# The first layer's gate: its last feature tile in two token halves, and an earlier split of the convolution's second weight tile

## The chip, the cores and the metric

One core of a Trainium2 chip runs the whole program. The metric is the device time of one execution in microseconds (us). The kernel before took 1762.61 us, the median of three runs from 1762.31 to 1763.01. The engines are TensorE (PE: matmuls, with weight loads in a queue of their own, PEld), VectorE (DVE), ScalarE (ACT), GpSimd (POOL) and SyncE (SP, which starts the DMA transfers). Each runs its own program in order, and they meet only through semaphores.

## The reference

The reference is a block with two attention branches and then two layers of a second block, on 512 tokens with 1024 features. The change lies at the end of the first of these two layers and the start of the next one's convolution:

```python
        f = sq_relu_mlp(rmsnorm_2(x, g[2]), w_mlp_up[i], w_mlp_down[i])
        x = x + rmsnorm_2(f, g[3])
        gate = jax.nn.sigmoid(rmsnorm_2(x, g[4]) @ w_ple_gate[i])     # 1024 x 1024
        e = (p[i] @ w_ple_proj[i]) * gate
        x = x + rmsnorm_2(e, g[5])
    # layer 1 then begins with rmsnorm_2(x, g[0]) @ w_conv_in (1024 x 3072)
```

`rmsnorm_2` divides each token by the root of the mean of its squares over all 1024 features. So `e` must be complete, in all features, before any token of `x` can be updated, and the convolution's matmuls begin only after that.

## The kernel before

**Layout.** Activations lie with the features on the 128 partitions and the 512 tokens along the free axis. 1024 features are 8 such tiles of 128x512 (`KT` = 8, `S` = 512, `P` = 128); `wt(k)` is tile k of the work buffer. `TOKENS` (L504) names the two token halves of 256 columns.

**Matmuls.** Float32 operands are split into a high and a low part (`fp32r`), and a product is three matmuls: high by high, high by low, low by high (`three`, L813 on; the matmuls are L816, L817 and L818). A weight unit is 1024 rows by 256 columns, in SBUF 128x2048. It comes in by one DMA, ACT copies out the high part, DVE subtracts it to get the low part ("the split"), and PE then makes two tiles of outputs from it (m = 0 and 1), each from 8 steps k of three matmuls. Raw and split weights have two slots each, used in turn. So the split of unit u waits until unit u-2 has been used up (`tile_done` against `pl.freed`), and the load of unit u waits until unit u-2 is split. A tile is made in one of four PSUM banks; `tile_done` counts finished tiles, `tile_read` counts those that have been read.

**The gate of layer 0** has four weight units (`ple_gate0`, 0 to 3). PE (`embed_gate`, L1279) makes units 0 and 1 in `first_units`, and units 2 and 3 in `project` (L921), a hardware loop of one pass; unit 3 goes tile by tile, all of m = 0 and then all of m = 1. For each tile DVE multiplies by the token's scale (`scaled`, L1999), ACT takes the sigmoid (L1848), DVE multiplies the embedding tile by it (L2593), ACT squares the product (L1424), and POOL adds the squares up (`sum_squares`, L2699; each addition is L2709). The eighth square goes around POOL: PE multiplies POOL's sum of seven by a matrix of ones (`begin_statistics`, L937, the matmul is L958) and then adds the eighth (`end_statistics`, L941, the matmul is L943), so that every partition has the sum. `keep_array_busy` (L947, the matmul is L949) issues filler matmuls whose result nobody reads: one between the two and five behind them. These matmuls are plain float32, and each leaves two records in the trace.

**What follows.** ACT loads the table for logarithm and exponential and turns the sum into the scale (`make_rstd`, L1480; L1483 and L1485). DVE and ACT then update x and make the inputs of the convolution (`add_normed`, L2025, in the order `CONV_NORM_ORDER`, L490; `norm_input`, L1431). The first tile goes in token halves. PE's `first_units` takes each tile as it comes, from both of the convolution's first weight units (`conv_in`, 0 and 1), first five steps k of both in turn (`FIRST_UNITS`, L496).

**The split of `conv_in` 1.** It is done in two halves of 1024 columns, so that PE can begin on the lower four steps k early. `conv_in` 1 uses the slot of `ple_gate0` 3, the gate's last unit. On ACT the first half is done in two quarters (`split_quarter`, L1874), of which the first waits until the gate's last unit is used up; they lie before and behind the sigmoid of the last tile. On DVE it comes when all eight gated tiles are done (`split_half`, L2598). The second half stands later, in the orders of the update.

The order of all this on each engine is written out by hand, in the program's order of instructions.

Of the kernel before, what the change touches and what calls it, by code (L numbers as in the profile page):

```python
# [21 lines left out]
P = 128  # L22
# [171 lines left out]
def hybrid_block_kernel(nc, ins, out):  # L194
# [4 lines left out]
    with ctx:  # L199
# [3 lines left out]
        def sem(name):  # L203
            return ctx.enter_context(nc.semaphore(name))
# [43 lines left out]
        def wt(i):  # L248

            return work[:, bass.ds(i * S, S)]  # L250
# [66 lines left out]
        conv_hi = sem("conv_hi")  # L317
        conv_ready = sem("conv_ready")
        gained = sem("gained")
        head_x = sem("head_x")  # L320
        head_hi = sem("head_hi")
        head_scaled = sem("head_scaled")
# [477 lines left out]
        def _(pe):  # L800
# [120 lines left out]
            def project(name, passes, x, ready=None, first=0):  # L921

                with pe.Fori(first, passes) as i:
                    for j in range(2):
                        unit(Place(tab, name, j, i, 2, passes), KT, 256, 2, x, ready if j == 0 else None, by_tile=j == 1)
# [15 lines left out]
            def end_statistics():  # L941
                pe.wait_ge(sq_done, n["squares"])
                nc.tensor.matmul(banks[7][:, :], ones, sq[:, (n["squares"] - 1) % 2, :], start=False, stop=True)\  # L943
                    .then_inc(stat_done, 1)
                n.add("stat")

            def keep_array_busy(*columns):  # L947
                for cols in columns:
                    nc.tensor.matmul(banks[6][:, 0:cols], ones, rope[:, 0:cols], start=True, stop=True)  # L949
# [329 lines left out]
            def embed_gate(layer):  # L1279
                embed_project(f"ple_gate{layer}", layer)  # L1280
                first_units(f"ple_gate{layer}", n.add("in", KT) - KT)
                if layer == 0:
                    project(f"ple_gate{layer}", 2, from_a, first=1)
                    begin_statistics()
                    keep_array_busy(S)
                    end_statistics()
                    keep_array_busy(S, S, S, S, S)
                    return

                x_tiles = iter(range(KT))  # L1290
                addends = iter(range(KT))

                def turn_x(tiles):
                    for _ in range(tiles):
                        turn_out(X + next(x_tiles))

                def turn_addend(tiles):
                    for _ in range(tiles):
                        k = next(addends)
                        pe.wait_ge(gained, k + 1)  # L1300
                        turn_out(EG + k)

# [12 lines left out]
                tokens_half(pl, 1, range(KT // 2))  # L1315
                turn_addend(1)
                tokens_half(pl, 1, range(KT // 2, KT))

                done = n.add("squares", KT)
                for half in range(2):  # L1320
                    pe.wait_ge(gained, KT + half)
                    turn_out(EG + KT - 1, half)
                    if half == 0:
                        pe.wait_ge(sq_added, n.add("sq", KT - 2))
                        pe.wait_ge(rstd_ready, n["stat"])
                        pe.wait_ge(sq_done, done)
                        token_sums(0, (0, 1, 2), pl)
                        token_sums(1, (0, 1), pl)
                    else:
                        pe.wait_ge(sq_done, done + 1)  # L1330
                        token_sums(1, (2,), pl)

            def tokens_half(pl, half, k_tiles):

# [18 lines left out]
            def token_sums(half, parts, pl):  # L1353

                at = token_sums_at(pl, half)
                for part in parts:
                    squares = (ssum[:, :], sq[:, 1 - LAST_SQUARE, :], sq[:, LAST_SQUARE, :])[part]
                    for a in (2 * half, 2 * half + 1):
                        mm = nc.tensor.matmul(at[:, a:a + 1], squares[:, a * P:(a + 1) * P], ones[:, 0:1],
                                              start=part == 0 and a == 2 * half, stop=part == 2 and a == 2 * half + 1)  # L1360
                if part == 2:
                    mm.then_inc(stat_done, 1)
# [17 lines left out]
        def _(act):  # L1380
# [23 lines left out]
            def split_half(name, j, half):  # L1404

                pl = Place(tab, name, j)
                cols = slice(half * UNIT // 2, (half + 1) * UNIT // 2)
                if name == "sb_qk" and half == 0:
                    act.wait_ge(half_landed, 16)
                else:  # L1410
                    act.wait_ge(raw_landed[pl.slot], pl.landed)
                if pl.freed is not None:
                    act.wait_ge(tile_done, pl.freed)
                nc.scalar.activation(wsp[:, pl.slot, 0, cols], raw[:, pl.slot, cols], ACT.Copy)\
                    .then_inc(w_hi if half else half_hi, 1)
# [416 lines left out]
            def embed_gate(layer):  # L1832
                name = f"ple_gate{layer}"
                for j in range(4):
# [11 lines left out]
                    def sigmoid(m):  # L1846
                        act.wait_ge(tile_read, pl.tile + m + 1)
                        nc.scalar.activation(tmp[:, 2 + m, :], tmp[:, m, :], ACT.Sigmoid).then_inc(gate_out, 1)  # L1848
# [22 lines left out]
                        act.wait_ge(ln_done, n["stat"])  # L1871
                        nc.scalar.activation(rstd_tok[:, tiles], rstd_tok[:, tiles], ACT.Exp, scale=-0.5).then_inc(rstd_ready, 1)

                    def split_quarter(quarter):  # L1874
                        following = Place(tab, "conv_in", 1)
                        if quarter == 0:
                            act.wait_ge(raw_landed[following.slot], following.landed)
                            act.wait_ge(tile_done, following.freed)
                        cols = slice(quarter * UNIT // 4, (quarter + 1) * UNIT // 4)
                        mm = nc.scalar.activation(wsp[:, following.slot, 0, cols], raw[:, following.slot, cols], ACT.Copy)  # L1880
                        if quarter == 1:
                            mm.then_inc(half_hi, 1)

                    if layer == 0 and j == 3:
                        sigmoid(0)
                        square_gated(0)
                        split_quarter(0)
                        sigmoid(1)
                        split_quarter(1)
                        square_gated(1)  # L1890
                        table("natural_log_exp_and_others")
                        break
                    if layer == 1 and j == 3:
                        sigmoid(0)
# [53 lines left out]
        def _(dve):  # L1948
# [623 lines left out]
            def embed_gate(layer):  # L2572
                name = f"ple_gate{layer}"
                for j in range(4):
                    pl = Place(tab, name, j)
                    if j == 0:
                        third_after_norm(name)
                        wait_rstd()
                    elif j > 1:
                        ahead(name, j)  # L2580
                    late = j == 3
                    scaled(tmp[:, 0, :], pl, 0)
                    if not late:
                        scaled(tmp[:, 1, :], pl, 1)
                    for m in range(2):
                        if late and m and layer == 1:
                            last_halves(pl)
                            return
                        if late and m:
                            scaled(tmp[:, 1, :], pl, 1)  # L2590
                        dve.wait_ge(gate_out, n.add("gate"))
                        k = 2 * j + m
                        V.tensor_tensor(wt(k), wt(k), tmp[:, 2 + m, :], ALU.mult).then_inc(gated, 1)  # L2593
                        if layer == 1:
                            dve.wait_ge(gated, KT + k + 1)
                            V.tensor_scalar(wt(EG + k), wt(k), col(G_NORM2 + 48 + 40 + k), None, ALU.mult).then_inc(gained, 1)
                dve.wait_ge(gated, KT * (layer + 1))
                split_half("conv_in", 1, 0)  # L2598
                add_normed(0, G_NORM2 + 40, G_NORM2 + 48, "conv_in")

            def last_halves(pl):
                k = KT - 1
# [178 lines left out]
```

## Time and profile before

| | before |
|---|---|
| device time, median of 3 runs | 1762.61 us (1762.31 to 1763.01) |
| the profiled execution, whole | 1762.93 us |
| its span, first to last instruction | 1761.2 us |
| TensorE matmul busy | 1738.8 us, 99% |
| VectorE busy | 1038.4 us, 59% |
| ScalarE busy | 740.9 us, 42% |
| GpSimd busy | 166.9 us, 9% |
| mean granted TensorE clock | 0.997 of full speed |

Busy time is what an engine spent in instructions, as a share of the span. Times in a timeline are from the span's start. Matmuls are pipelined: their records overlap, and the time that one costs in a row of them is the distance from start to start. An idle time in brackets is that of the engine just before the instruction, with what ended it.

### The profile page before, as it was taken

The page shows a single profiled execution, that of the slowest core. Times are in us where ns is not written, and L with a number is a line of the kernel's source. Part 1 is how long each engine was busy: PE and PEld are TensorE (multiplying, and loading weights), DVE is VectorE, ACT ScalarE, POOL GpSimd, SP SyncE. Part 2 cuts the span into 40 slices and gives each one's busy share as a digit, 9 for nine tenths or more (in the row PEclk, how much of TensorE's full clock was granted, in tenths as well). Part 3 has the DMA queues.
Part 4 walks back from the last instruction along what each step waited for, and adds up shares of the span by engine and source line. Part 5 has one row for each costly group of instructions (what it writes and reads, how often), then busy time and mean ns, then how long its engine had stood idle before and what let it go on. Part 6 is the DMA issues. An engine that isn't in the chain of part 4 may idle for free.

```text
span 1761.2 us, 21949 instructions
## 1 busy us (share of the span) xinstructions
PE 1738.8 (99%) x8325; PEld 1432.0 (81%) x8325; DVE 1038.4 (59%) x1422; ACT 740.9 (42%) x1090; POOL 166.9 (9%) x145
## 2 busy tenths in 40 slices
PE   9999999999999999999999999999999999999997
PEld 7988877888788887788888888768887888888876
DVE  6478876776557776573535354775566544444456
ACT  4266764665426666441212123642225222222345
POOL 2011112000300000210000001320003000000031
PEclk9999999999999999999999999999999999999999
DMA  8222123214233222223222323213332332322321
GB/s 270 80 65 72 49 66 94 73 48 144 72 106 75 72 73 79 72 96 96 96 97 94 100 93 106 94 63 113 103 101 68 108 96 96 96 95 96 108 73 48
DMA packets 165543, 160.36 MB, mean 91 GB/s; under 512 B 13929, under 2 KB 158854, under 8 KB 165206
## 3 DMA queue, kind: packets, MB, share of 16 engines
q1 hardware_dynamic: 165302, 159.19, 28.9%
q8 instruction: 54, 0.88, 0.2%
q14 instruction: 27, 0.22, 0.0%
q10 hardware_dynamic: 160, 0.07, 0.0%
HBM read 150.43 MB, written 4.19 MB: 88 GB/s over the span
## 4 chain that ended last, share of the span: by engine, by line
PE 94%; DVE 3%; ACT 2%; issue 0%; DVEq 0%; ACTq 0%
PE bank L816 29%; PE bank L818 29%; PE bank L817 29%; PE bank L1120 2%; PE bank L1138 1%; PE bank L1045 1%; PE bank L958 1%; PE bank L1034 1%; DVE act_a L2009 1%; ACT act_a L1437 1%; DVE work L2035 1%; PE bank L1350 0%; PE bank L943 0%; PE bank L974 0%; DVE bank L2030 0%
## 5 line engine op out<-in xcount | busy, mean ns | idle before, releaser
L816 PE MATMUL bank<-act_a,split_weights 128*128 128x512 f32 (+1 forms) x1400 | 555.3, 397 | 3.7 <-DVE split_weights L2007 1.3
L818 PE MATMUL bank<-act_a,split_weights 128*128 128x512 f32 (+1 forms) x1400 | 544.7, 389 | 0.0
L817 PE MATMUL bank<-act_a,split_weights 128*128 128x512 f32 (+1 forms) x1400 | 544.5, 389 | 0.0
L1392 ACT ACTIVATE split_weights<-raw_weights 128x2048 fp32r<-128x2048 f32 x116 | 221.4, 1909 | 344.8 <-PE bank L818 344.8
L1961 DVE TENSOR_TENSOR split_weights<-raw_weights,split_weights 128x2048 fp32r<-128x2048 f32 x116 | 267.6, 2307 | 119.8 <-ACT split_weights L1392 116.5
L816 PEld LDWEIGHTS bank<-act_a,split_weights 128*128 128x128 f32 x1400 | 263.1, 188 | 63.3 <-issue 8.1
L818 PEld LDWEIGHTS bank<-act_a,split_weights 128*128 128x128 f32 x1400 | 262.5, 187 | 56.0
L817 PEld LDWEIGHTS bank<-act_a,split_weights 128*128 128x128 f32 x1400 | 262.9, 188 | 52.8 <-issue 1.7
L816 PE MATMUL bank<-act_b,split_weights 128*128 128x512 f32 x664 | 259.2, 390 | 0.0
L817 PE MATMUL bank<-act_b,split_weights 128*128 128x512 f32 x664 | 258.3, 389 | 0.0
L818 PE MATMUL bank<-act_b,split_weights 128*128 128x512 f32 x664 | 258.3, 389 | 0.0
L817 PEld LDWEIGHTS bank<-act_b,split_weights 128*128 128x128 f32 x664 | 124.6, 188 | 26.2 <-issue 0.5
L816 PEld LDWEIGHTS bank<-act_b,split_weights 128*128 128x128 f32 x664 | 124.6, 188 | 26.2 <-issue 0.5
L818 PEld LDWEIGHTS bank<-act_b,split_weights 128*128 128x128 f32 x664 | 124.6, 188 | 26.0
L2713 POOL TENSOR_TENSOR ssum<-sq 128x512 f32<-128x512 f32 x16 | 23.4, 1463 | 1223.6 <-ACT sq L1424 1220.3
L1805 ACT ACTIVATE act_b<-tmp 128x512 fp32r<-128x512 f32 x64 | 40.3, 632 | 227.5 <-DVE tmp L2545 226.1
L1424 ACT ACTIVATE sq<-work 128x512 f32<-128x512 f32 x116 | 71.5, 625 | 146.5 <-DVE work L2562 58.8
L2545 DVE SCALAR_TENSOR_TENSOR tmp<-bank,rstd 128x512 f32<-128x512 f32 x64 | 43.6, 691 | 133.1 <-PE bank L818 133.1
L2709 POOL TENSOR_TENSOR ssum<-ssum,sq 128x512 f32<-128x512 f32 x77 | 105.4, 1369 | 144.8 <-ACT sq L1424 139.8
L2562 DVE TENSOR_TENSOR work<-bank,work 128x512 f32<-128x512 f32 x48 | 32.9, 692 | 124.1 <-PE bank L818 124.1
L2007 DVE TENSOR_TENSOR act_b<-tmp,act_b 128x512 fp32r<-128x512 f32 (+3 forms) x144 | 82.5, 610 | 6.0 <-ACT act_b L538 5.1
L2007 DVE TENSOR_TENSOR act_b<-bank,act_b 128x128 fp32r<-128x128 f32 (+1 forms) x96 | 45.3, 485 | 23.8 <-ACT act_b L1692 23.5
(228 smaller groups left out, 2013.7 us busy)
## 6 DMA issues: line engine op xcount, KB each, us to landing
raw_weights<-in_w_mlp_up SPq DMA_DIRECT2D x32, 1024.0 KB, 5.4
raw_weights<-in_w_mlp_down SPq DMA_DIRECT2D x32, 1024.0 KB, 5.2
raw_weights<-in_w_in SPq DMA_DIRECT2D x18, 1024.0 KB, 5.3
raw_weights<-in_w_conv_in SPq DMA_DIRECT2D x12, 1024.0 KB, 5.1
raw_weights<-in_w_attn_in SPq DMA_DIRECT2D x16, 512.0 KB, 4.6
raw_weights<-in_w_ple_gate SPq DMA_DIRECT2D x8, 1024.0 KB, 5.1
raw_weights<-in_w_out SPq DMA_DIRECT2D x4, 1024.0 KB, 5.2
raw_weights<-in_w_attn_in SPq DMA_DIRECT2D x4, 1024.0 KB, 5.2
```

The costliest lines, as they stand in the source:

```text
L816: nc.tensor.matmul(dst, w[0], a[0], start=first, stop=False)
L817: nc.tensor.matmul(dst, w[0], a[1], start=False, stop=False)
L818: mm = nc.tensor.matmul(dst, w[1], a[0], start=False, stop=last)
L1120: return nc.tensor.matmul(dst, qk(a)[0:rows, j * P:(j + 1) * P], qk(b)[0:rows, 0:cols], start=first, stop=last)
L1392: nc.scalar.activation(wsp[:, pl.slot, 0, :], raw[:, pl.slot, :], ACT.Copy)\
L1424: nc.scalar.activation(sq[:, parity, :], src, ACT.Square).then_inc(sq_done, 1)
L1805: nc.scalar.activation(act_b[:, 0, 2 * j + m, :], tmp[:, m, :], ACT.Square)\
L1961: V.tensor_tensor(wsp[:, pl.slot, 1, :], raw[:, pl.slot, :], wsp[:, pl.slot, 0, :].bitcast(F32), ALU.subtract).then_inc(w_split, 1)
L2007: V.tensor_tensor(dst, src, hi.bitcast(F32), ALU.subtract).then_inc(sem_, 1)
L2545: V.scalar_tensor_tensor(out=tmp[:, m, :], in0=done(pl, m)[:, :], scalar=0.0, in1=rstd[:, :], op0=ALU.max, op1=ALU.mult).then_inc(tile_rea ...
L2562: V.tensor_tensor(t, done(pl, m)[:, :], t, ALU.add).then_inc(tile_read, 1)
L2709: nc.gpsimd.tensor_tensor(ssum[:, :], ssum[:, :], sq[:, parity, :], ALU.add).then_inc(sq_added, 1)
```

## The change

- PE: unit 2 of the gate is made by `unit` directly, without the hardware loop. Unit 3 is made by `gate_in_halves`: tile m = 0 whole, then tile m = 1 in two token halves, in two banks. For the steps k = 0 to 5 the halves alternate, then come k = 6, 7 of the first half and k = 6, 7 of the second. Three semaphores are raised there: `gate_used` when k = 3 of the second half is done (the lower half of the weight slot isn't needed any more), `half_tile` at the end of the first half, `tile_done` at the end of the second.
- PE: the filler between the two parts of the column sum has 256 columns instead of 512, and the last square is added in two halves (`end_in_halves`).
- ACT: the first half of `conv_in` 1's split is one instruction of 1024 columns, ahead of the sigmoid of tile 6, and waits for `gate_used`. The last tile's sigmoid is taken in halves, and of its square ACT makes the first half.
- DVE: its part of that split stands ahead of the scaling of tile 6. The last tile is scaled and multiplied in halves, and DVE makes the second half of the square.

```diff
                 if layer == 0:
-                    project(f"ple_gate{layer}", 2, from_a, first=1)
+                    unit(Place(tab, "ple_gate0", 2), KT, 256, 2, from_a)
+                    gate_in_halves(Place(tab, "ple_gate0", 3))
                     begin_statistics()
-                    keep_array_busy(S)
-                    end_statistics()
+                    keep_array_busy(S // 2)
+                    end_in_halves()
                     keep_array_busy(S, S, S, S, S)
                     return
...
+            def gate_in_halves(pl):
+                pe.wait_ge(w_split, pl.u + 1)
+                def piece(k, m, b, cols, done=None):
+                    c = k * 256 + m * P
+                    three(bank(pl, b)[:, cols], [weights(pl, hl, c, c + P) for hl in (0, 1)],
+                          [act_a[:, hl, k, cols] for hl in (0, 1)], k == 0, k == KT - 1, done)
+                empty(pl.tile, 0)
+                for k in range(KT):
+                    piece(k, 0, 0, slice(0, S), tile_done if k == KT - 1 else None)
+                for half in range(2):
+                    empty(pl.tile, 1 + half)
+                pieces = [(half, k) for k in range(KT - 2) for half in range(2)]
+                pieces += [(half, k) for half in range(2) for k in range(KT - 2, KT)]
+                for half, k in pieces:
+                    done = {(1, KT // 2 - 1): gate_used, (0, KT - 1): half_tile, (1, KT - 1): tile_done}
+                    piece(k, 1, 1 + half, TOKENS[half], done.get((half, k)))
+            def end_in_halves():
+                squares = sq[:, (n["squares"] - 1) % 2, :]
+                for half in range(2):
+                    if half:
+                        pe.wait_ge(sq_done, n["squares"])
+                    else:
+                        pe.wait_ge(half_square, 1)
+                    mm = nc.tensor.matmul(banks[7][:, TOKENS[half]], ones, squares[:, TOKENS[half]], start=False, stop=half == 1)
+                mm.then_inc(stat_done, 1)
...
   (ACT, split_half)
-                if pl.freed is not None:
+                if name == "conv_in" and half == 0:
+                    act.wait_ge(gate_used, 1)
+                elif pl.freed is not None:
                     act.wait_ge(tile_done, pl.freed)
...
   (ACT, embed_gate; split_quarter is removed)
                     if layer == 0 and j == 3:
+                        split_half("conv_in", 1, 0)
                         sigmoid(0)
                         square_gated(0)
-                        split_quarter(0)
-                        sigmoid(1)
-                        split_quarter(1)
-                        square_gated(1)
+                        act.wait_ge(half_scaled, 1)
+                        nc.scalar.activation(tmp[:, 3, TOKENS[0]], tmp[:, 1, TOKENS[0]], ACT.Sigmoid).then_inc(half_sigmoid, 1)
+                        act.wait_ge(tile_read, pl.tile + 2)
+                        nc.scalar.activation(tmp[:, 3, TOKENS[1]], tmp[:, 1, TOKENS[1]], ACT.Sigmoid).then_inc(gate_out, 1)
+                        act.wait_ge(half_gated, 1)
+                        act.wait_ge(sq_added, n["added"] + KT - 2)
+                        nc.scalar.activation(sq[:, (n["squares"] + KT - 1) % 2, TOKENS[0]], wt(KT - 1)[:, TOKENS[0]], ACT.Square)\
+                            .then_inc(half_square, 1)
                         table("natural_log_exp_and_others")
...
   (DVE, embed_gate)
                     late = j == 3
+                    if late and layer == 0:
+                        split_half("conv_in", 1, 0)
                     scaled(tmp[:, 0, :], pl, 0)
...
                         if late and m:
-                            scaled(tmp[:, 1, :], pl, 1)
+                            gate_halves(pl)
+                            break
...
-                split_half("conv_in", 1, 0)
                 add_normed(0, G_NORM2 + 40, G_NORM2 + 48, "conv_in")
+            def gate_halves(pl):
...
+                scaled_half(0)      # waits for half_tile, 256 columns
+                scaled_half(1)      # waits for tile_done
+                gated_half(0)       # waits for half_sigmoid
+                gated_half(1)       # waits for gate_out
+                dve.wait_ge(gated, KT)
+                dve.wait_ge(half_square, 1)
+                V.tensor_tensor(sq[:, LAST_SQUARE, TOKENS[1]], wt(k)[:, TOKENS[1]], wt(k)[:, TOKENS[1]], ALU.mult)\
+                    .then_inc(sq_done, 1)
```

## Rows read from the trace of the kernel before

**Rows 1.** Page, busy us of each engine, share of the span, instructions.
```profile
PE 1738.8 (99%) x8325; PEld 1432.0 (81%) x8325; DVE 1038.4 (59%) x1422; ACT 740.9 (42%) x1090; POOL 166.9 (9%) x145
```

**Rows 2.** Page, the chain that ended last, by engine.
```profile
PE 94%; DVE 3%; ACT 2%; issue 0%; DVEq 0%; ACTq 0%
```

**Rows 3.** Timeline of PE around the hole: start us, duration us, engine, line, operands.
```profile
1140.04 0.39 PE L816 MATMUL bank<-act_a,split_weights 128*128 128x512 f32 x1
...
1145.25 0.39 PE L818 MATMUL bank<-act_a,split_weights 128*128 128x512 f32 x1
1145.92 1.12 PE L958 MATMUL bank<-ssum,consts 128*128 128x512 f32 x2 [0.29 <-POOL ssum L2709]
...
1148.47 1.13 PE L943 MATMUL bank<-sq,consts 128*128 128x512 f32 x2 [0.56 <-ACT sq L1424]
1149.43 4.45 PE L949 MATMUL bank<-consts 128*128 128x512 f32 x10
1154.04 0.47 PE L816 MATMUL bank<-act_a,split_weights 128*128 128x512 f32 x1 [0.16 <-DVE act_a L2009]
```

**Rows 4.** Timeline of DVE in the same stretch.
```profile
1141.77 0.68 DVE L1999 TENSOR_TENSOR tmp<-bank,rstd 128x512 f32<-128x512 f32 x1
...
1145.67 0.69 DVE L1999 TENSOR_TENSOR tmp<-bank,rstd 128x512 f32<-128x512 f32 x1 [1.84 <-PE bank L818]
...
1147.79 1.22 DVE L1981 TENSOR_TENSOR split_weights<-raw_weights,split_weights 128x1024 fp32r<-128x1024 f32 x1
```

**Rows 5.** Timeline of ACT in the same stretch.
```profile
1142.48 0.63 ACT L1848 ACTIVATE tmp<-tmp 128x512 f32<-128x512 f32 x1 [3.13 <-DVE tmp L1999]
1143.87 0.63 ACT L1424 ACTIVATE sq<-work 128x512 f32<-128x512 f32 x1 [0.76 <-DVE work L2593]
...
1147.79 0.63 ACT L1424 ACTIVATE sq<-work 128x512 f32<-128x512 f32 x1 [0.24 <-DVE work L2593]
1148.43 1.28 ACT L1384 ACT_TABLE_LOAD   x1
1149.73 0.66 ACT L1483 ACTIVATE bank<-bank,eps 128x512 f32<-128x512 f32 x1
```

**Rows 6.** Timeline of POOL, 1125 to 1166: beside a quiet and a busy DVE.
```profile
1144.58 1.29 POOL L2709 TENSOR_TENSOR ssum<-ssum,sq 128x512 f32<-128x512 f32 x1 [4.88 <-ACT sq L1424]
...
1162.57 1.55 POOL L2709 TENSOR_TENSOR ssum<-ssum,sq 128x512 f32<-128x512 f32 x1 [0.16 <-POOL ssum L2709]
```

**Rows 7.** Timeline of PE in the second layer's gate, matmuls of 256 columns.
```profile
1743.15 0.28 PE L817 MATMUL bank<-act_a,split_weights 128*128 128x256 f32 x1
...
1745.42 0.28 PE L818 MATMUL bank<-act_a,split_weights 128*128 128x256 f32 x1
```

**Rows 8.** Lines L1981 and L1414, halves of a split: ns min/median/max, first, last.
```profile
L1981 DVE TENSOR_TENSOR split_weights<-raw_weights,split_weights x15: 1214/1226/1872, 13.5 to 1701.2; 128x1024 fp32r<-128x1024 f32 x15
L1414 ACT ACTIVATE split_weights<-raw_weights x14: 1039/1043/1071, 12.0 to 1700.1; 128x1024 fp32r<-128x1024 f32 x14
```

**Rows 9.** Timeline of DVE in the second layer's gate, 256 columns.
```profile
1745.74 0.42 DVE L2606 TENSOR_TENSOR tmp<-bank,rstd 128x256 f32<-128x256 f32 x1 [1.57 <-PE bank L818]
```

**Rows 10.** Line L1857, ACT's sigmoid of 256 columns there.
```profile
L1857 ACT ACTIVATE tmp<-tmp x2: 407/412/417, 1746.2 to 1750.4; 128x256 f32<-128x256 f32 x2
```

**Rows 11.** Windows: length, busy PE, PEld, DVE, ACT, POOL, granted clock, DMA, GB/s.
```profile
674.00:676.00 2.00, 0.81 (x4) 0.68 (x5) 1.97 (x4) 1.98 (x4) 0.00 (x0) 1.00 0.00 0
678.00:680.00 2.00, 0.54 (x4) 0.24 (x3) 1.15 (x3) 1.92 (x5) 0.00 (x0) 1.00 1.05 365
680.00:682.00 2.00, 1.70 (x7) 1.23 (x8) 2.00 (x5) 1.93 (x5) 0.00 (x0) 0.85 0.06 19
682.00:684.00 2.00, 2.00 (x7) 1.56 (x6) 1.97 (x4) 2.00 (x6) 0.00 (x0) 0.50 0.58 129
684.00:686.00 2.00, 2.00 (x10) 1.59 (x10) 1.97 (x6) 1.84 (x4) 0.00 (x0) 0.80 0.02 6
```

**Rows 12.** Timeline of PE in the convolution's opening, its one longer wait.
```profile
1163.01 0.50 PE L816 MATMUL bank<-act_a,split_weights 128*128 128x512 f32 x1 [0.40 <-DVE act_a L2009]
```

More of the change, by code:

```diff
@@ L319, in hybrid_block_kernel @@
         gained = sem("gained")
+        gate_used = sem("gate_used")
+        half_tile = sem("half_tile")
+        half_scaled = sem("half_scaled")
+        half_sigmoid = sem("half_sigmoid")
+        half_gated = sem("half_gated")
+        half_square = sem("half_square")
         head_x = sem("head_x")
@@ L1331, in embed_gate @@
                         token_sums(1, (2,), pl)
+            def gate_in_halves(pl):
[23 more added lines that the diff above has]
+                mm.then_inc(stat_done, 1)
+                n.add("stat")
             def tokens_half(pl, half, k_tiles):
@@ L1872, in token_rstd @@
                         nc.scalar.activation(rstd_tok[:, tiles], rstd_tok[:, tiles], ACT.Exp, scale=-0.5).then_inc(rstd_ready, 1)
[L1874 to L1882, printed above, removed]
                     if layer == 0 and j == 3:
+                        split_half("conv_in", 1, 0)
                         sigmoid(0)
                         square_gated(0)
-                        split_quarter(0)
-                        sigmoid(1)
-                        split_quarter(1)
-                        square_gated(1)
+                        act.wait_ge(half_scaled, 1)
[6 more added lines that the diff above has]
+                            .then_inc(half_square, 1)
                         table("natural_log_exp_and_others")
+                        n.add("gated")
                         break
@@ L2597, in embed_gate, with scaled_half, gated_half @@
                 dve.wait_ge(gated, KT * (layer + 1))
-                split_half("conv_in", 1, 0)
                 add_normed(0, G_NORM2 + 40, G_NORM2 + 48, "conv_in")
+            def gate_halves(pl):
+                k = KT - 1
+                def scaled_half(half):
+                    cols = TOKENS[half]
+                    if half:
+                        dve.wait_ge(tile_done, pl.tile + 2)
+                    else:
+                        dve.wait_ge(half_tile, 1)
+                    V.tensor_tensor(tmp[:, 1, cols], banks[(pl.bank + 1 + half) % 4][:, cols], rstd[:, cols], ALU.mult)\
+                        .then_inc(tile_read if half else half_scaled, 1)
+                def gated_half(half):
+                    cols = TOKENS[half]
+                    if half:
+                        dve.wait_ge(gate_out, n.add("gate"))
+                    else:
+                        dve.wait_ge(half_sigmoid, 1)
+                    V.tensor_tensor(wt(k)[:, cols], wt(k)[:, cols], tmp[:, 3, cols], ALU.mult)\
+                        .then_inc(gated if half else half_gated, 1)
+                scaled_half(0)
[6 more added lines that the diff above has]
+                    .then_inc(sq_done, 1)
             def last_halves(pl):
```

## The prediction

> **What bounds the kernel now.** I read four views, from coarse to fine. The page's busy table comes first: TensorE is busy 99% of the span [rows 1], so the kernel can only get shorter where TensorE has a hole, and anything that widens a hole is paid in full. The chain that ended last says the same: PE carries 94% of it, DVE 3%, ACT 2% [rows 2]. The change touches the hole between the first layer's gate and the convolution, so the next view is the timeline of that stretch, engine by engine. On PE the last matmul of the gate starts at 1145.25 and lasts 0.39, so the gate ends at 1145.64; the first matmul of the convolution starts at 1154.04 [rows 3]. The 8.4 us between hold only the two column sums for the normalization (L958, L943) and fillers (L949).
>
> What sets those 8.4 us is one relay: DVE scales the last tile (1145.67, 0.69) [rows 4], ACT takes the sigmoid, DVE multiplies, ACT squares (1147.79, 0.63) [rows 4, 5], PE adds the square into the sum (1148.47, 1.13, end 1149.60) [rows 3]. Beside it ACT loads a table (1148.43, 1.28, end 1149.71), then the logarithm starts at 1149.73 [rows 5]. From there to the first convolution matmul it is 4.31 us that the change leaves alone. The other input of the sum is early: tile 6 is scaled at 1141.77 [rows 4], gets its sigmoid at 1142.48 and its square at 1143.87 [rows 5], and POOL adds it at 1144.58, 1.29 us, so to 1145.87 [rows 6]. L958 starts 0.05 later, at 1145.92. So tile 6 arrives just as the gate ends, with nearly no slack. The half split of the convolution's second weight tile costs nothing now: DVE does it at 1147.79 [rows 4] and then has to wait for the logarithm anyway.
>
> **The change, part by part.** The sum is made against the profiled execution, 1762.93 us (span 1761.2), which is 0.32 above the median of 1762.61.
>
> PE, the tile in halves. Start-to-start, 512-column matmuls take 0.2265 us (23 steps from 1140.04 to 1145.25) [rows 3] and 256-column ones 0.1195 (19 steps from 1743.15 to 1745.42) [rows 7]. The last tile goes from 24 x 0.2265 to 48 x 0.1195, 5.44 to 5.74: PE pays 0.30 us. The tile still begins at 1140.04. The 24th small matmul (gate_used) starts at 1140.04 + 23 x 0.1195 = 1142.79 and ends 0.28 later, 1143.07; the 42nd (half_tile) ends at 1145.22; the 48th at 1145.94. Half 0 is so 0.42 us earlier and half 1 0.30 later than the whole tile was.
>
> A page puts the small matmul otherwise. The Trainium skill, "TensorE: Matmul & The Clock Gate", section "Back-to-back issue gap", has 256 columns at 256 cycles plus a small floor, 109 ns, where the row has 119.5. By it the tile would end 0.5 us sooner and gate_used come 0.25 sooner, and by that rule the total below would be 0.25 smaller; the measured row decides.
>
> Loop removed. Before, PE enters this part through a hardware loop of one pass. I take 0 for its removal, with 0 to 0.1 us of gain as bounds: PE goes on at its even pitch inside it, and the exit lies in the wait for POOL [rows 3].
>
> ACT and DVE, the split that moves. This is the part that decides. It used to stand on DVE behind all of the gate, and on ACT in two quarters beside the last tile's relay. Now ACT has it ahead of sigmoid(0), behind the wait for gate_used, and DVE has it ahead of scaled(0), behind ACT's half. Tile 6 has been ready since 1140.2, but both engines that must treat it stand behind that wait. The queue, with durations from rows: ACT's 1024 columns take 1.043 [rows 8], so 1143.10 to 1144.14; DVE's take 1.226 [rows 8], so 1144.17 to 1145.39. Back to back DVE starts 0.07 before the end of its predecessor, so scaled(0) is 1145.32 to 1146.01 (0.69), where it was 1141.77 to 1142.45 [rows 4]. Sigmoid 0.63 [rows 5]: 1146.67. Multiply 0.69: 1147.39. Square 0.63: 1148.06. POOL's add starts 0.08 later (as from 1144.50 to 1144.58): 1148.14, and takes 1.29 when DVE is quiet or 1.55 beside a busy DVE [rows 6]. DVE is half busy here, with the half tiles' operations, so I take 1.4: 1149.54. L958 starts at about 1149.6, where it was 1145.92.
>
> The half tiles meanwhile. 256-column operations take 0.42 on DVE [rows 9] and 0.412 on ACT [rows 10]. Both scaled halves end at 1148.2; half the sigmoids at 1148.44 and 1148.8; the products at 1148.9 and 1149.3; ACT's half square at 1149.35 and DVE's at 1149.8. The table load then ends at 1150.6. All of it is ready before PE asks for it, so the halves lie entirely behind tile 6. That cover hides the new DVE square (0.42) and the extra instruction starts.
>
> PE behind it. L958 to the next instruction 0.96, as from 1148.47 to 1149.43 [rows 3]. A filler of 512 columns is two records at 0.43 apart [rows 3], one of 256 then 0.43 in all. The first half of the last sum 0.43, the second 0.22 to its last record, which lasts 0.38. Together 2.41: the sum ends at 1152.0. The logarithm starts at 1152.05 instead of 1149.73: **2.3 us later**. The five fillers (4.45 us from 1149.43 [rows 3]) shift with it and end 0.05 ahead of the convolution's first matmul, now 1156.35. No DMA moves with the split: SP waits for the second half's split, which stays where it was.
>
> The new stall and the clock. From the end of the gate at 1145.94 PE has nothing until 1149.6, 3.6 us, since no filler stands there. In the whole trace the granted clock fell once before the end: PE is busy 0.54 of the 2 us from 678, then the clock is 0.85, 0.50 and 0.80 over the next three stretches of 2 us [rows 11]. That is 0.6 + 2.0 + 0.8 = 3.4 us at 1.2 GHz instead of 2.4 GHz, after a stall of less than 2 us. The new stall is twice as long, so I expect the fall. While PE works at the lower level it loses half of the time, at most 1.7 us. If the fall begins within the stall, part of the low stretch is idle anyway, and the loss goes down to about 1.0. What falls on the fillers delays only PE and not DVE's chain; a wait of 0.40 us in the convolution's opening [rows 12] gives some of that back. I take 1.3 between the ends 0.7 and 1.7.
>
> The Trainium skill, "TensorE: Matmul & The Clock Gate", section "HAM oscillation — how this bites in real kernels", says that idle gaps between bursts of matmuls put the clock back and make the next burst start cold. By that rule this change pays twice, for the wait and for the clock; the trace agrees, with 0.50 granted behind its own longest hole [rows 11].
>
> Sum: 2.3 + 1.3 = 3.6 us. 1762.93 + 3.6 = 1766.5 for an execution like the profiled one, 1766.2 from the median.
>
> **The rivals.**
> - The clock doesn't fall, or not in most executions. For it: PE is busy only 0.81 of the 2 us from 674, and the clock stayed at 1.00 [rows 11], so it matters how a stall lies. Against it: this one is longer than any in the trace. Then only the wait is paid: 1762.61 + 2.3 = 1764.9.
> - The other side: the halves win. This needs tile 6 out of the way. Then half 1, done at 1145.94, goes through 0.42 + 0.41 + 0.42 + 0.42 and four handovers to 1147.75, its sum to 1148.4, and the table load, now behind half a square, ends at 1148.5: the logarithm 1.2 us sooner, 1761.4. The point from which it decides: gate_used to L958 is a relay of 6.5 us, and L958 may start at 1147.3 at the latest for the sum to end at 1149.7 as now. So gate_used would have to come by 1140.8, in the first five of 48 small matmuls; it stands behind the 24th. Only if the split on ACT and DVE cost much less than rows 8 have it, or were passed by the tile's own work, could it be. The program order speaks against it.
> - The moves cancel: what is lost ahead of L958 comes back after it, in the convolution's opening, so that nothing is seen: 1762.6. Against it: the whole DVE and ACT chain of the opening hangs on the logarithm, and PE's wait there is on that chain [rows 12].
> - Worse: POOL is slowed to 1.55, and the low clock is granted a second time, because the array has a hole at its start as well. Another 1.7: 1767.9.
>
> **How the numbers follow.** Forecast with a fall of the clock 0.62, no fall 0.22, halves win 0.06, cancel 0.04, worse 0.06. The predicted time is that of the forecast, 1766.2; its own range is 1765.6 to 1766.8. The range reaches down into the no-fall case and up to where a slower POOL lands: 1764.4 to 1767.3. 0.2% of the time, about what a measurement of this kernel can tell from no change, is 3.5 us, so the forecast lies just over that border: two thirds of its chance are slower (0.42), with the worst case 0.48; one third, the no-fall case and the cancelling one are the same, 0.46; faster 0.06.
>
> **What would show it.** In the profile after: DVE's half split ahead of the first scaling, at about 1144.2; scaled(0) near 1145.3 and not 1141.8; POOL's last add near 1148.1; L958 near 1149.6 with an idle time of over 3 us before it; the logarithm near 1152 and the first convolution matmul 2 to 4 us later than 1154.04; a granted clock under 1.00 somewhere from 1148 to 1154, and fillers 0.86 apart in it instead of 0.43. It is wrong if scaled(0) still starts near 1142, if L958 starts before 1147.3, or if the hole is the same and the time isn't.

## The result, and the profile after

The changed kernel takes 1766.55 us (median of nine runs, 1765.71 to 1767.81), against 1762.61 for the kernel before run beside it. The ratio is 1.0023, with a 95% interval of 1.0014 to 1.0031: about 3.9 us slower. The profiled execution took 1766.01 us with a span of 1764.0. TensorE has the same busy time as in [rows 1], so what came on is, taken together, waiting (the matmuls that ran slow behind the new hole are made up for by faster ones near 680, as shown below):

```profile
PE 1738.9 (99%) x8351; PEld 1434.2 (81%) x8351; DVE 1039.7 (59%) x1425; ACT 740.0 (42%) x1090; POOL 166.8 (9%) x145
```

The timeline of PE from the first small matmul of the last tile to the first of the convolution, which answers to [rows 3]. Line numbers have moved: L816 to L818 are now L822 to L824, L958 is L964, L943 is L1367, L949 is L955.

```profile
1139.50 0.28 PE L822 MATMUL bank<-act_a,split_weights 128*128 128x256 f32 x1
...
1145.13 0.28 PE L824 MATMUL bank<-act_a,split_weights 128*128 128x256 f32 x1
1149.00 1.13 PE L964 MATMUL bank<-ssum,consts 128*128 128x512 f32 x2 [3.59 <-POOL ssum L2778]
1149.96 0.83 PE L955 MATMUL bank<-consts 128*128 128x256 f32 x2
1150.58 1.91 PE L1367 MATMUL bank<-sq,consts 128*128 128x256 f32 x4
1152.29 5.11 PE L955 MATMUL bank<-consts 128*128 128x512 f32 x10
1156.92 0.72 PE L822 MATMUL bank<-act_a,split_weights 128*128 128x512 f32 x1
```

The idle time in brackets is the new wait, 3.59 us, for POOL. It is followed back through POOL, DVE and ACT. DVE, to be set against [rows 4]:

```profile
1143.73 1.23 DVE L2017 TENSOR_TENSOR split_weights<-raw_weights,split_weights 128x1024 fp32r<-128x1024 f32 x1 [2.42 <-ACT split_weights L1454]
1144.87 0.68 DVE L2035 TENSOR_TENSOR tmp<-bank,rstd 128x512 f32<-128x512 f32 x1
1146.25 0.69 DVE L2632 TENSOR_TENSOR work<-work,tmp 128x512 f32<-128x512 f32 x1 [0.69 <-ACT tmp L1888]
```

ACT, to be set against [rows 5]:

```profile
1142.63 1.06 ACT L1454 ACTIVATE split_weights<-raw_weights 128x1024 fp32r<-128x1024 f32 x1 [3.82 <-PE bank L824]
1145.59 0.63 ACT L1888 ACTIVATE tmp<-tmp 128x512 f32<-128x512 f32 x1 [1.89 <-DVE tmp L2035]
1146.98 0.63 ACT L1464 ACTIVATE sq<-work 128x512 f32<-128x512 f32 x1 [0.76 <-DVE work L2632]
...
1152.54 0.66 ACT L1523 ACTIVATE bank<-bank,eps 128x512 f32<-128x512 f32 x1 [1.55 <-PE bank L1367]
```

POOL's last addition, to be set against [rows 6]:

```profile
1147.68 1.26 POOL L2778 TENSOR_TENSOR ssum<-ssum,sq 128x512 f32<-128x512 f32 x1 [8.53 <-ACT sq L1464]
```

Each row waits for the one before it in the chain: ACT stood idle 3.82 us until PE had marked the lower half of the weight slot, DVE stood 2.42 us until ACT had split it, and only then was tile 6 scaled. In the kernel before, ACT and DVE had begun with tile 6 by then. The windows across the hole, with the granted clock third from the right:

```profile
1146.00:1148.00 2.00, 0.00 (x0) 0.00 (x0) 1.41 (x4) 1.24 (x4) 0.32 (x1) 1.00 0.00 0
1148.00:1150.00 2.00, 1.00 (x3) 0.52 (x4) 1.78 (x3) 0.94 (x3) 0.95 (x1) 1.00 0.00 0
1150.00:1152.00 2.00, 2.00 (x7) 1.62 (x6) 0.21 (x1) 0.98 (x1) 0.00 (x0) 0.55 0.00 0
1152.00:1154.00 2.00, 2.00 (x5) 1.07 (x4) 0.09 (x1) 1.24 (x2) 0.00 (x0) 0.60 0.00 0
```

0.55 and 0.60 are 1.8 and 1.6 us at 1.2 GHz: a low stretch of 3.4 us behind the hole. The first matmul of the sum still has its full speed (1.13 us, 1.12 before); the middle filler, the last square and the first fillers behind it are slow.

Executions differ in where they begin, so all comparisons below count from the start of the last tile's second half (in the kernel before: of tile m = 1), in us:

| | L958 (POOL's sum) | logarithm | first convolution matmul | low clock behind the hole |
|---|---|---|---|---|
| before | 5.88 | 9.69 | 14.00 | none |
| the change | 9.50 | 13.04 | 17.42 | 3.4 us |
| difference | +3.62 | +3.35 | +3.42 | |

3.42 us more here, but the span is only 2.8 us longer. The profiled execution of the change escaped the fall near 680 that [rows 11] show, and its last tile began 0.54 us sooner: 3.42 - 0.54 = 2.88. PE's wait in that older hole is the same 1.76 us, first in the kernel before, then in the change, whose clock stays at 1.00 behind it:

```profile
680.30 0.33 PE L1138 MATMUL bank<-consts,tmp 128*128 128x128 f32 x1 [1.76 <-ACT tmp L1675]
680.84 0.33 PE L1144 MATMUL bank<-consts,tmp 128*128 128x128 f32 x1 [1.76 <-ACT tmp L1715]
680.00:682.00 2.00, 1.16 (x6) 0.85 (x7) 1.94 (x6) 1.93 (x5) 0.00 (x0) 1.00 0.40 126
```

From there to the last tile it is 459.74 us in the kernel before and 458.66 in the change, so the fall near 680 costs about 1.1 us where it happens. With it, this execution would have taken about 1767.1 us.

### The profile page after: what moved, and what is told of

It reads as the page before. It is cut to its first block, busy times and chain, and to the rows that moved or that the text cites. A ratio compares the mean times of both kernels' runs of the same rounds, so it can differ in the third digit from the quotient of the medians.

```text
span 1764.0 us, 22003 instructions
## 1 busy us (share of the span) xinstructions
PE 1738.9 (99%) x8351; PEld 1434.2 (81%) x8351; DVE 1039.7 (59%) x1425; ACT 740.0 (42%) x1090; POOL 166.8 (9%) x145
## 4 chain that ended last, share of the span: by engine, by line
PE 93%; DVE 4%; ACT 2%; issue 0%; DVEq 0%; POOL 0%; ACTq 0%
PE bank L822 29%; PE bank L824 28%; PE bank L823 28%; PE bank L1126 2%; PE bank L1144 1%; PE bank L1051 1%; PE bank L964 1%; PE bank L1040 1%; DVE act_a L2045 1%; ACT act_a L1477 1%; DVE work L2071 1%; PE bank L1388 0%; PE bank L949 0%; PE bank L980 0%; DVE bank L2066 0%
## 5 line engine op out<-in xcount | busy, mean ns | idle before, releaser
L822 PE MATMUL bank<-act_a,split_weights 128*128 128x512 f32 (+1 forms) x1408 | 556.5, 395 | 3.7 <-DVE split_weights L2043 1.3
L824 PE MATMUL bank<-act_a,split_weights 128*128 128x512 f32 (+1 forms) x1408 | 545.7, 388 | 0.0
L822 PEld LDWEIGHTS bank<-act_a,split_weights 128*128 128x128 f32 x1408 | 264.3, 188 | 62.5 <-issue 7.5
L824 PEld LDWEIGHTS bank<-act_a,split_weights 128*128 128x128 f32 x1408 | 263.7, 187 | 55.8
L822 PE MATMUL bank<-act_b,split_weights 128*128 128x512 f32 x664 | 259.3, 390 | 0.0
L824 PE MATMUL bank<-act_b,split_weights 128*128 128x512 f32 x664 | 258.4, 389 | 0.0
L822 PEld LDWEIGHTS bank<-act_b,split_weights 128*128 128x128 f32 x664 | 124.6, 188 | 26.1 <-issue 0.5
L824 PEld LDWEIGHTS bank<-act_b,split_weights 128*128 128x128 f32 x664 | 124.6, 188 | 26.0
```

The lines of the kernel that those rows point to most:

```text
L822: nc.tensor.matmul(dst, w[0], a[0], start=first, stop=False)
L824: mm = nc.tensor.matmul(dst, w[1], a[0], start=False, stop=last)
```

## The experiments

The runs form three groups, each on a chip of its own beside runs of the kernel before: experiments 1 to 4 (its median there is 1762.42), 5 and 6 (1762.94), and 7 and 8 (1762.48). Times of different groups are compared by what each is above or below the kernel before in its own group. Times within a profile count from the start of the last tile's second half, as above.

**1. The halves, with the split behind them.** Of the change only the place of the split is undone: on ACT it is still one instruction, now behind tile 6's square, and on DVE it stands behind the gate again.

```diff
 (ACT)  if layer == 0 and j == 3:
-           split_half("conv_in", 1, 0)
            sigmoid(0)
            square_gated(0)
+           split_half("conv_in", 1, 0)
            act.wait_ge(half_scaled, 1)
 (DVE)  late = j == 3
-       if late and layer == 0:
-           split_half("conv_in", 1, 0)
...
        dve.wait_ge(gated, KT * (layer + 1))
+       split_half("conv_in", 1, 0)
        add_normed(0, G_NORM2 + 40, G_NORM2 + 48, "conv_in")
```

> The changed kernel with the convolution's half split put where neither engine holds tile 6 back: on ACT between the square of tile 6 and the first half sigmoid, on DVE behind all of the gate as before. Theory (the moved split is the loss, the halves themselves are a gain): scaling of tile 6 back at about 1.7 us behind the start of the last tile, column sum started within 0.1 us of the tile's end, logarithm 1.1 us sooner than in the kernel before: 1761.4 us, 1.2 below before and about 5 below the change. Rival 1 (the halves, with 24 more matmuls and more instructions, are the loss): it stays above 1763. Rival 2 (the clock alone is the loss and the order doesn't matter): 1765 or more.

Measured: 1761.40 us (1761.06 to 1762.14), ratio to before 0.9994, interval 0.9985 to 1.0003. PE, then ACT:

```profile
1140.07 0.28 PE L822 MATMUL bank<-act_a,split_weights 128*128 128x256 f32 x1
...
1145.96 1.13 PE L964 MATMUL bank<-ssum,consts 128*128 128x512 f32 x2
1146.93 0.59 PE L955 MATMUL bank<-consts 128*128 128x256 f32 x2
1147.36 1.21 PE L1367 MATMUL bank<-sq,consts 128*128 128x256 f32 x4
...
1152.92 0.47 PE L822 MATMUL bank<-act_a,split_weights 128*128 128x512 f32 x1
```

```profile
1144.44 1.04 ACT L1454 ACTIVATE split_weights<-raw_weights 128x1024 fp32r<-128x1024 f32 x1
1145.76 0.42 ACT L1919 ACTIVATE tmp<-tmp 128x256 f32<-128x256 f32 x1 [0.28 <-DVE tmp L2647]
...
1148.61 0.66 ACT L1523 ACTIVATE bank<-bank,eps 128x512 f32<-128x512 f32 x1
```

The sum begins at 5.89 again, and the logarithm at 8.54 instead of 9.69: 1.15 us sooner. ACT's split now ends 0.28 us before the first half sigmoid can start, in time that was idle. So the halves are a gain, and the 24 extra matmuls are not the loss. Nor is the hardware loop that went: with the same fall near 680, the last tile begins at 1140.07 here and at 1140.04 in the kernel before. The same kernel run again (experiment 7) gave 1761.59.

**2. The split alone, with the tile whole.** The kernel before, with ACT's and DVE's part of the split placed as in the change.

```diff
 (PE)   if layer == 0:
-           project(f"ple_gate{layer}", 2, from_a, first=1)
+           unit(Place(tab, "ple_gate0", 2), KT, 256, 2, from_a)
+           gate_marked(Place(tab, "ple_gate0", 3))
...
+    def gate_marked(pl):
+        pe.wait_ge(w_split, pl.u + 1)
+        for m in range(2):
+            empty(pl.tile, m)
+            for k in range(KT):
+                c = k * 256 + m * P
+                done = tile_done if k == KT - 1 else gate_used if (m, k) == (1, KT // 2 - 1) else None
+                three(bank(pl, m)[:, :], [weights(pl, hl, c, c + P) for hl in (0, 1)],
+                      [from_a(hl, k) for hl in (0, 1)], k == 0, k == KT - 1, done)
 (ACT)  if layer == 0 and j == 3:
+           split_half("conv_in", 1, 0)      # waits for gate_used
            sigmoid(0)
            square_gated(0)
-           split_quarter(0)
            sigmoid(1)
-           split_quarter(1)
            square_gated(1)
 (DVE)  late = j == 3
+       if late and layer == 0:
+           split_half("conv_in", 1, 0)
        scaled(tmp[:, 0, :], pl, 0)
...
        dve.wait_ge(gated, KT * (layer + 1))
-       split_half("conv_in", 1, 0)
        add_normed(0, G_NORM2 + 40, G_NORM2 + 48, "conv_in")
```

> The kernel before, tile whole, with the split alone moved: on ACT ahead of the sigmoid of tile 6 behind a wait for the lower half of the weight slot, on DVE ahead of the scaling of tile 6. Theory: the mark comes with the 12th of 24 matmuls, 2.9 us into the tile, so tile 6 is held back as in the change, and tile 7 in one piece comes out later than in halves: logarithm 2.6 us later than before, plus some 1.3 for the clock, 1766.5 us, as slow as the change or a little slower. Rival 1 (the halves are the loss): 1762.6, as before. Rival 2 (clock alone): also near the change, since the hole is there; this run doesn't tell it apart.

Measured: 1767.43 us (1766.94 to 1767.94), ratio 1.0029, interval 1.0018 to 1.0039. PE, then the logarithm on ACT:

```profile
1149.40 2.07 PE L959 MATMUL bank<-ssum,consts 128*128 128x512 f32 x2 [3.74 <-POOL ssum L2724]
1151.27 1.73 PE L950 MATMUL bank<-consts 128*128 128x512 f32 x2
1152.83 1.02 PE L944 MATMUL bank<-sq,consts 128*128 128x512 f32 x2
1153.89 0.66 ACT L1498 ACTIVATE bank<-bank,eps 128x512 f32<-128x512 f32 x1 [2.03 <-PE bank L944]
```

The wait is there without any halves, 3.74 us. The two records of POOL's sum (L959) last 2.07 instead of 1.12 [rows 3]: here it ran at the low clock from its start, and the filler behind it too. The logarithm is at 13.83, 4.14 us behind the kernel before. At full speed the way from POOL's sum to it would be 2.9 us (0.96 + 0.86 + 1.06) instead of 4.49, so 2.5 of the 4.14 are the wait, as expected, and 1.6 are the clock, where 1.3 was expected. The rest of the 0.9 us by which the median lies above the expected time isn't explained: the fall near 680 is in this profile, but also in that of the kernel before. With experiment 1 this settles the first half of the cause: the moved split is the loss, and the halves take a part of it back.

**3. Fillers in the hole.**

```diff
                     gate_in_halves(Place(tab, "ple_gate0", 3))
+                    keep_array_busy(S, S, S, S)
                     begin_statistics()
```

> The change with four more filler matmuls of 512 columns between the end of the gate and the column sum, 3.4 us in the hole of 3.6. Theory: the granted clock stays at 1.00 there, the wait stays: logarithm 2.3 to 2.4 us later than in the kernel before instead of 3.35, 1765.0 us, and with less spread between executions than the change had (1765.7 to 1767.8). Rival 2 (the clock is all of the loss): 1762.6. If the clock costs nothing: 1766.5.

Measured: 1764.74 us (1764.52 to 1765.03), ratio 1.0013, interval 1.0004 to 1.0022. PE, then ACT:

```profile
1145.48 3.60 PE L955 MATMUL bank<-consts 128*128 128x512 f32 x8
1149.23 1.13 PE L964 MATMUL bank<-ssum,consts 128*128 128x512 f32 x2 [0.15 <-POOL ssum L2779]
```

```profile
1151.69 0.66 ACT L1524 ACTIVATE bank<-bank,eps 128x512 f32<-128x512 f32 x1 [0.48 <-PE bank L1368]
```

```profile
1150.00:1152.00 2.00, 2.00 (x9) 1.41 (x8) 0.43 (x1) 1.52 (x2) 0.00 (x0) 1.00 0.00 0
```

The granted clock is 1.00 in this window and in all others from 1144 to 1160. The sum still begins at 9.51, so the order of the engines is untouched, and the logarithm comes at 11.97, 1.07 us sooner than in the change. 2.28 us of the loss are the wait. This kernel is 2.3 us above the kernel before run beside it, the change was 3.9 above: the rest, 1.6 us, went with the low clock. The spread is 0.5 us instead of 2.1, but that of the kernel before is 1.7 in this group, so the spread shows little by itself.

**4. DVE's part back, ACT's part left early.** The DVE lines of experiment 1's diff alone.

> The change with DVE's part of the split back behind the gate, ACT's part left ahead of the sigmoid of tile 6. Tells DVE's queue from ACT's. Theory: tile 6 is scaled early, its sigmoid waits for ACT's split, 4.1 us into the last tile; POOL's last addition ends 7.5 us into the tile, the column sum starts 1.7 later than before, and the logarithm only 0.3 later, since the halves take 1.2 back: 1762.9 us, up to 1763.9 if the clock still falls behind the shorter hole. Rival (ACT's wait is the whole of the loss): 1766.

Measured: 1763.04 us (1762.40 to 1763.55), ratio 1.0003, interval 0.9994 to 1.0012. ACT, then PE:

```profile
1143.02 1.06 ACT L1454 ACTIVATE split_weights<-raw_weights 128x1024 fp32r<-128x1024 f32 x1 [3.82 <-PE bank L824]
1143.99 0.62 ACT L1888 ACTIVATE tmp<-tmp 128x512 f32<-128x512 f32 x1
```

```profile
1147.39 1.13 PE L964 MATMUL bank<-ssum,consts 128*128 128x512 f32 x2 [1.59 <-POOL ssum L2777]
```

Tile 6's sigmoid now follows straight behind ACT's split, and the sum begins at 7.50. So of the 3.6 us by which it was late, ACT's place makes 1.6 and DVE's 2.0. The halves give back most of what ACT's place costs: the logarithm is at 9.96, 0.27 behind the kernel before. The clock is 1.00 in all windows around this hole of 1.59 us; two of the eleven executions have a mean clock of 0.996, so that it falls there in some isn't excluded.

**5. The change once more.** No edit.

> The changed kernel once more, to see whether its two groups of times (1765.7 to 1766.1 and 1767.3 to 1767.8) come again and what differs in the trace. Theory: the clock falls behind the new hole in all of them; the slower group has one more low stretch, behind the older hole in the last pairs of attention heads (1.76 us, near 680) or directly behind the first one, so its mean granted clock is lower by 0.001 to 0.002. Median 1766.0 to 1767.3. Rival (the groups are something other than the clock): equal clocks in both.

Measured: 1767.33 us (1765.80 to 1767.99), ratio 1.0026, interval 1.0016 to 1.0036. This profiled execution, 1767.99 us, is one of the upper group. PE, ACT, and the windows:

```profile
1140.29 0.28 PE L822 MATMUL bank<-act_a,split_weights 128*128 128x256 f32 x1
...
1149.79 2.08 PE L964 MATMUL bank<-ssum,consts 128*128 128x512 f32 x2 [3.59 <-POOL ssum L2778]
...
1158.85 0.64 PE L822 MATMUL bank<-act_a,split_weights 128*128 128x512 f32 x1
```

```profile
1154.46 0.66 ACT L1523 ACTIVATE bank<-bank,eps 128x512 f32<-128x512 f32 x1 [2.70 <-PE bank L1367]
```

```profile
680.00:682.00 2.00, 1.49 (x6) 0.95 (x7) 1.97 (x5) 1.90 (x6) 0.00 (x0) 0.73 0.22 65
1148.00:1150.00 2.00, 0.21 (x1) 0.21 (x2) 1.67 (x4) 1.00 (x3) 1.26 (x1) 0.64 0.00 0
1150.00:1152.00 2.00, 2.00 (x3) 0.96 (x4) 0.77 (x3) 1.70 (x2) 0.00 (x0) 0.50 0.00 0
1152.00:1154.00 2.00, 2.00 (x6) 1.56 (x5) 0.00 (x0) 0.00 (x0) 0.00 (x0) 0.50 0.00 0
1154.00:1156.00 2.00, 2.00 (x4) 1.00 (x4) 0.16 (x1) 1.24 (x2) 0.00 (x0) 0.66 0.00 0
```

The wait is the same 3.59 us and the sum begins at the same 9.50, but the clock falls within the hole and stays low for 1.4 + 2 + 2 + 1.4 = 6.8 us, twice as long. The logarithm comes at 14.17 and the convolution at 18.56, 1.14 later than in the first profile. The fall near 680 is there too, behind the same 1.76 us, and the tile began 0.79 later. Together 1.93 of the 1.98 us between the two executions. Of the 18 executions of this kernel 13 lie above 1766.5, with mean clocks of 0.995 or 0.996, and five between 1765.7 and 1766.2, with 0.997. 3.4 us at half speed take about 0.001 off the mean clock of such a span, so the upper group has one or two low stretches more. The groups are the clock's. Which stretch each of them has is known only for the two that were profiled.

**6. Two fillers in the hole.** As experiment 3, with `keep_array_busy(S, S)`.

> The change with two filler matmuls of 512 columns (1.7 us) in the hole instead of none or four. Theory: the order of the engines is the same, so only the clock differs. With the hole cut to about 1.9 us, as long as the one near 680, the clock falls in some executions and not in others: times between those with four fillers (1764.7) and the change (1766.5), some near the one and some near the other, or 1764.7 throughout if two are enough. If the fall depended on PE being idle before the sum at all, it would be 1766.5.

Measured: 1765.02 us (1764.33 to 1766.06), ratio 1.0014, interval 1.0005 to 1.0023. PE:

```profile
1145.39 1.88 PE L955 MATMUL bank<-consts 128*128 128x512 f32 x4
1149.14 1.12 PE L964 MATMUL bank<-ssum,consts 128*128 128x512 f32 x2 [1.87 <-POOL ssum L2779]
```

A wait of 1.87 us is left, and the sum runs at the high clock here. The median is 2.1 us above the kernel before run beside it, where four fillers had 2.3, and 2.3 below the change in the same group (experiment 5): two fillers took the clock's part away as well as four did. The times reach up to 1766.06, a spread of 1.7 us, but that of the kernel before beside it is 1.5, and a fall near 680, which this profile escaped, can make up 1.1 of it. Whether the clock still falls at the new hole in some executions is open; no profile shows it.

**7 and 8. The best version again, and without its middle filler.** The second takes `keep_array_busy(S // 2)` out of experiment 1's kernel.

> The version with the halves and the split behind them (k1_behind) once more, since its gain of 1.0 us was smaller than its interval. Theory: 1.0 to 1.2 us below the kernel before run beside it. Rival (the first result was chance): no difference.

> The same version without the filler of 256 columns between POOL's sum and the halves of the last square. Theory: PE reaches the first half 0.43 us sooner, but the second half's square (DVE, 1.85 us behind the tile's end) sets the end of the sum, so the logarithm comes 0 to 0.1 us sooner and the time is the same within 0.1 us; the filler is covered. If the filler is on the path: 0.4 us less. The clock shouldn't fall for so short a hole.

Measured: 1761.59 us (1761.16 to 1762.18), ratio 0.9995, interval 0.9985 to 1.0004, and 1761.36 us (1760.55 to 1762.12), ratio 0.9993, interval 0.9984 to 1.0002. PE and ACT of the second:

```profile
1145.20 1.12 PE L964 MATMUL bank<-ssum,consts 128*128 128x512 f32 x2
1146.51 1.28 PE L1366 MATMUL bank<-sq,consts 128*128 128x256 f32 x4 [0.19 <-ACT sq L1923]
```

```profile
1147.83 0.66 ACT L1522 ACTIVATE bank<-bank,eps 128x512 f32<-128x512 f32 x1
```

With the start of the half tile at 1139.30 the logarithm is at 8.53, as with the filler (8.54): the filler is covered, PE then waits for the squares. The gain over the kernel before is 0.9 to 1.1 us in all three sets of runs (experiments 1, 7 and 8), near the 1.15 us in the traces. But each interval includes 1, so by the runs alone it isn't clear of noise.

## Why the prediction was right, and where it was off

**The moved split holds tile 6 back: right.** Predicted from the start of the half tile (1140.04 there): scaling of tile 6 at 5.28, measured 5.37; POOL's addition at 8.10, measured 8.18; the sum at 9.50 to 9.56, measured 9.50. That the last one fits so well is partly luck: the steps before POOL came 0.08 to 0.09 late, and POOL's addition was 0.14 shorter than taken. From the first small matmul's start to the last one's it was 5.63, where 47 steps of [rows 7] had given 5.62. The two handovers before the scaling are what makes it late, and experiments 1, 2 and 4 show it from three sides.

**The halves lie behind tile 6: right.** Without a low clock the logarithm comes 2.28 us late (experiment 3), where 2.3 was forecast. From the logarithm to the convolution 4.31 us were to stay as they were; they are 4.38. The 1.2 us that the halves would win with tile 6 out of the way were 1.15 in experiment 1. The other side's rival was a real mechanism, and failed here at the point named: `gate_used` came behind the 24th small matmul.

**POOL beside a busy DVE: the wrong engine pays.** I raised POOL's addition from 1.29 to 1.4, after [rows 6]. It took 1.26. DVE's first half product, which began 0.27 behind it, took 1.28 us instead of 0.42 and ended 0.29 behind its end (line L2657 of the change; the second took 0.41, and in experiment 1, where POOL had finished, both took 0.42):

```profile
L2657 DVE TENSOR_TENSOR work<-work,tmp x2: 411/848/1284, 1147.9 to 1149.2; 128x256 f32<-128x256 f32 x2
```

It cost nothing, since the halves had slack behind POOL's sum: DVE's half of the square ended at 1150.20, and PE took up the last square at 1150.58.

**The clock falls: right, with its size and its chances off.** In the first profile it took 3.54 - 2.46 = 1.08 us from the sum to the logarithm (experiment 3 has 2.46), within the 0.7 to 1.7 given. The Trainium skill ("TensorE: Matmul & The Clock Gate", section "HAM oscillation — how this bites in real kernels") says that an idle gap makes the next burst of matmuls start cold. The runs agree that this is a cost of its own: with POOL's sum as late as in the change, the time is 1.6 us less against the kernel before when fillers stand in the gap (experiment 3), and 2.3 less in the group of experiments 5 and 6. But a second low stretch, given 0.06, is what experiment 5 profiled (without the slower POOL that the same rival had), and the upper group, with more low clock than one fall at this hole gives, holds 13 of 18 executions. The case without a fall, given 0.22, is by the times in none of the 18: the lowest, 1765.71, is above all of experiment 3's.

The forecast 1766.2 was 0.35 under the median of the first nine runs and 1.1 under that of the second nine, which lies just outside the range given (1764.4 to 1767.3), on a chip where the kernel before is 0.3 slower too. That the first median is so near is in part luck: the forecast lies between the two groups, the first median is the lowest time of the upper one, and the profiled execution came below 1766.5 only because it escaped the fall near 680. What was mis-sized is the term for the clock, 1.3 us: it is 1.6 in the first nine (3.9 above the kernel before, less the 2.3 of experiment 3), and 2.1 to 2.3 in the second nine (4.4 less 2.3, or against the two fillers beside it). How much of this is the fall near 680, which comes in some executions of every kernel here, is open. I had priced one low stretch and had argued about where in the sum it lies, not that a fall which begins inside the hole can be followed directly by another.

## What to carry to other kernels

Work that "has to be done sometime" isn't free earlier: on an engine that runs in order, moving it up means that everything queued behind it inherits its wait, so write down what each engine has ready at that moment before you put a waiting instruction there. A gain made shorter by pipelining in halves shows only if the other inputs of the same sum are on time. A new hole on TensorE can have two prices, as the one of 3.6 us had here: its own length and the slow clock behind it. Fillers in the hole took the second away, and a run of a kernel with fillers tells the two apart.

## What the runs showed of the hardware

- A 3.6 us hole on TensorE was followed by 3.4 us at 1.2 GHz in one execution and by 6.8 us in another of the same program, with the same order and waits. The times of the program come in two groups, 1.5 us apart.
- The same wait of 1.76 us near 680 was followed by a fall of the clock in 7 of the 10 profiled executions and not in the other three (the change, experiments 6 and 7), with the same order of work. From that hole to the last tile it took 459.65 to 459.78 us with the fall and 458.66 to 458.72 without, so it costs about 1.1 us. Before two single profiles are compared, look which of them has it.
- A DVE product of 256 columns in SBUF took 1.28 us beside a POOL addition, three times its 0.42, while the addition took 1.26, no more than alone (1.29 to 1.30). The product ended 0.29 us behind the addition, as if most of it had waited for the addition's end; that it waits is argued, not shown. In [rows 6] an addition beside a busy DVE took 1.55.
- Extra falls leave a mark in each execution's mean clock (0.997 against 0.995 or 0.996), which told the groups apart without a trace of each.
